# Thirty-two turns of the identity ahead of the input, the gate item in two products, one gate item in a bank of its own, and four changes of order

## The reference, cut to what matters

```python
def reference(x, mem, g_mix, w_in, b_igate, b_fgate, conv_w, conv_b, ...):
    ...
        xn = _rmsnorm(h, g_mix[l])
        proj = xn @ w_in[l]
        (sb_q, sb_k, sb_v, ml_q, ml_k, ml_v, ml_i, ml_f, ml_o, mem_q, gate_pre) = jnp.split(proj, splits, axis=-1)
        y_sb = _stick_breaking(...)
        qk = jax.nn.silu(_causal_conv(jnp.concatenate([ml_q, ml_k], axis=-1), conv_w[l], conv_b[l]))
        ...
        ig = (ml_i + b_igate[l]).astype(jnp.float32).transpose(0, 2, 1)
        lf = jax.nn.log_sigmoid((ml_f + b_fgate[l]).astype(jnp.float32)).transpose(0, 2, 1)
        hm = _mlstm(qh, kh, vh, ig, lf)
        ...
        gates = jax.nn.sigmoid(gate_pre + b_gate[l]).reshape(bsz, s, N_BRANCH, D_MODEL)
        ...
        h = h + merged @ w_out[l]
        hn = _rmsnorm(h, g_ffn[l])
        h = h + _peer(hn, w_peer_q[l], peer_k1[l], peer_k2[l], peer_u[l], peer_v[l])
```

## Time and profile before

| | us |
|---|---|
| median of 3 runs | 1645.74 |
| lowest, highest | 1645.55, 1647.4 |
| the profiled execution | 1646.79 |
| its span in the trace | 1645.1 |

### The profile page before, as it was taken

How to read it: one execution, slowest core, us unless ns; L and a number is a source line. 1 busy time by engine, 2 the same in 40 slices (tenths; PEclk the granted TensorE clock), 3 DMA queues, 4 the chain that set the end, 5 groups by cost and what they waited for, 6 DMA issues and landing times.

```text
span 1645.1 us, 23706 instructions
## 1 busy us (share of the span) xinstructions
PE 1629.1 (99%) x8192; PEld 1348.7 (82%) x8192; DVE 1085.2 (66%) x1884; ACT 755.4 (46%) x939; POOL 413.9 (25%) x180
## 2 busy tenths in 40 slices
...
DMA packets 165970, 344.39 MB, mean 209 GB/s; under 512 B 13068, under 2 KB 78604, under 8 KB 163600
## 3 DMA queue, kind: packets, MB, share of 16 engines
...
## 4 chain that ended last, share of the span: by engine, by line
PE 97%; DVE 1%; POOL 1%; DMA 0%; ACT 0%; issue 0%; SPq 0%; ACTq 0%
PE ps L971 28%; PE ps L962 27%; PE ps L634 19%; PE ps L647 9%; PE ps L885 4%; PE ps L1000 3%; PE ps L622 1%; PE ps L757 1%; POOL u_r L444 1%; PE ps L925 1%; PE ps L741 1%; PE ps L767 1%; PE ps L803 1%; PE ps L793 1%; PE ps L867 0%; PE ps L834 0%
## 5 line engine op out<-in xcount | busy, mean ns | idle before, releaser
L971 PE MATMUL ps<-v_r,w_pairs 128*128 128x512 f32 x2036 | 461.7, 389 | 0.0
L971 PEld LDWEIGHTS ps<-v_r,w_pairs 128*128 128x128 f32 x2036 | 382.1, 188 | 79.4
L962 PE MATMUL ps<-hT_r,u_r 128*128 128x512 f32 x1024 | 400.9, 391 | 0.5 <-POOL u_r L444 0.5
L962 PE MATMUL ps<-x_two,u_r 128*128 128x512 f32 x1024 | 398.7, 389 | 0.0
L419 POOL TENSOR_TENSOR w_r<-w_raw,w_r 128x1024 fp32r<-128x1024 f32 x93 | 234.8, 2527 | 396.1 <-ACT w_r L1097 390.3
L1903 DVE TENSOR_TENSOR v_r<-vraw,v_r 128x1024 fp32r<-128x1024 f32 x128 | 156.9, 1226 | 150.6 <-ACT v_r L1378 150.6
L1378 ACT ACTIVATE v_r<-vraw 128x1024 fp32r<-128x1024 f32 x128 | 135.7, 1060 | 253.9 <-PE ps L971 249.1
L634 PE MATMUL ps<-xT_r,w_r 128*128 128x512 f32 x984 | 230.2, 392 | 1.8 <-DVE xT_r L1419 1.0
L962 PEld LDWEIGHTS ps<-hT_r,u_r 128*128 128x128 f32 x1024 | 192.2, 188 | 41.2 <-POOL u_r L444 1.3
L962 PEld LDWEIGHTS ps<-x_two,u_r 128*128 128x128 f32 x1024 | 192.3, 188 | 39.4
L634 PEld LDWEIGHTS ps<-xT_r,w_r 128*128 128x128 f32 x984 | 182.9, 188 | 41.3 <-issue 2.4
...
## 6 DMA issues: line engine op xcount, KB each, us to landing
uraw<-in_u SPq DMA_DIRECT2D x128, 512.0 KB, 4.8
vraw<-in_v SPq DMA_DIRECT2D x128, 512.0 KB, 5.1
w_raw<-in_w SPq DMA_DIRECT2D x101, 512.0 KB, 3.5
acts_out<-act_stage SPq DMA_DIRECT2D x128, 256.0 KB, 2.3
...
act_in<-acts_out SPq DMA_DIRECT2D x128, 256.0 KB, 5.0
...
```

The lines of the kernel that those rows point to most:

```text
L962: ins = pe.matmul(bank(s % 2), u2[s][:, w, k * P:(k + 1) * P], x2[:, k, :] if w else hr4[:, 0, k, :], start=i == 0, stop=i == 15, skip_gro ...
L971: ins = pe.matmul(bank(2 * q + h), w2[:, s, w, q * P:(q + 1) * P], v2[s][:, w, h * BANK:(h + 1) * BANK], start=start and w == 0, stop=stop ...
```

## The change

Eight things change. `a`: ahead of the wait for x TensorE turns the identity 32 times into bank 7 (`WARM_TURNS`). `b`: the low part of item 0 is made by VectorE, behind the scaling of x, and both parts of item 1 by GpSimd, behind that; ScalarE no longer copies item 1. `c`: in item 16 GpSimd writes the low parts of the eight gate columns into unused columns (64 and 96 on) of the high part, so that high and low weights are one operand; TensorE does 16 matmuls in place of 24, and the sums over low weights come out in rows 64 to 67 and 96 to 99 of the same bank; ScalarE copies three rows of four out of the bank in place of one, and VectorE adds twice. `d`: the low part of item 17 is made by VectorE, ahead of the gate rows. `e`: the high part of item 19 is copied ahead of the Ln of the gate rows, not behind it. `f`: gate item 5 writes bank 6 and does not wait for item 4 to be taken out of bank 7. `g`: ScalarE takes an Exp of one column ahead of the first pair's scores, and the Exp of `r_m` stands behind the first pair. `h`: in the first `four_hots` the `low_u` stands behind all four groups of one-hots, not behind two. The other lines of the diff are counts and loops that follow from these.

```diff
+WARM_TURNS = 32
...
-DVE_LOW = tuple(I_KV + d for d in (1, 2, 4, 5, 7, 8, 10, 11))
+GATE_ASIDE = 5
...
+def gate_bank(m):
...
+    return 6 if m == GATE_ASIDE else 7
...
+DVE_LOW = (0, I_IF + 1) + tuple(I_KV + d for d in (1, 2, 4, 5, 7, 8, 10, 11))
...
-                        pool.wait_ge(w_hi_ready, o * 4 + (n + 1))
+                        pool.wait_ge(w_hi_ready, o * 4 + n)
...
-            low_ws(0, I_KV + 1)
+            pool.wait_ge(w_in[1], 16)
+            pool.wait_ge(w_lo_dve, 1)
+            pool.tensor_copy(wr4[:, 1, 0, :], raw3[:, 1, :]).then_inc(w_one_hi, 1)
+            pool.wait_ge(w_one_hi, 1)
+            pool.tensor_tensor(wr4[:, 1, 1, :], raw3[:, 1, :], wr4[:, 1, 0, :].bitcast(F32),
+                               ALU.subtract).then_inc(w_lo_ready, 1)
+            low_ws(2, I_IF - 2)
+            pool.wait_ge(w_hi_ready, I_IF)
+            raw_k = raw3[:, I_IF % 4, :].rearrange("p (k c) -> p k c", c=P)
+            hi_k = wr4[:, I_IF % 2, 0, :].rearrange("p (k c) -> p k c", c=P)
+            for i, done in ((0, if_low), (32, w_lo_ready)):
+                pool.tensor_tensor(hi_k[:, :, 64 + i:64 + i + MLH], raw_k[:, :, i:i + MLH],
+                                   hi_k[:, :, i:i + MLH].bitcast(F32), ALU.subtract).then_inc(done, 1)
+            low_ws(I_IF + 2, I_KV - 1 - I_IF)
...
-            with sp.Fori(1, I_IF // 4) as i:
+            for n in range(4, 8):
+                load_item(n, n % 4)
+            with sp.Fori(2, I_IF // 4) as i:
                 for s in range(4):
                     load_item(i * 4 + s, s)
-            for s in range(4):
-                load_item(I_IF + s, s)
-            with sp.Fori((I_IF + 4) // 4, (I_KV - 1) // 4) as i:
+            for n in range(I_IF, I_IF + 8):
+                load_item(n, n % 4)
+            with sp.Fori((I_IF + 8) // 4, (I_KV - 1) // 4) as i:
                 for s in range(4):
-                    load_item(i * 4 + s, s, 1)
+                    load_item(i * 4 + s, s, 1, 2)
...
             pe.wait_ge(const_set, CONSTS)
             pe.wait_ge(const_made, 4)
 
+            for i in range(WARM_TURNS):
+                turn(bank(7)[:, 0:P], ident[:, :])
...
             pe.wait_ge(proj_out, I_IF - 3)
-            t_item(I_IF, 0, 0, xr4)
+            take_item(I_IF)
+            pe.wait_ge(if_low, 1)
+            for k in range(KD):
+                for wa in range(2):
+                    ins = pe.matmul(bank(0), wr4[:, I_IF % 2, 0, k * P:(k + 1) * P], xr4[:, wa, k, :],
+                                    start=k == 0 and wa == 0, stop=k == KD - 1 and wa == 1)
+            ins.then_inc(item_done, 1)
...
-                at_least(pe, pre_out, m)
+                at_least(pe, pre_out, m - (m == GATE_ASIDE))
                 n = gate_at(m)
-                t_item(n, n % 2, 7, xr4)
+                t_item(n, n % 2, gate_bank(m), xr4)
...
             high_w(0, 0)
-            high_w(1, 1)
...
             act.wait_ge(item_done, I_N)
-            act.activation(r_zero, bank(0)[32:32 + MLH, :], ACT.Copy).then_inc(f_row, 1)
-            act.wait_ge(f_row, 1)
+            for dst, at in ((r_zero, 32), (r_f, 96), (r_max, 64)):
+                act.activation(dst, bank(0)[at:at + MLH, :], ACT.Copy).then_inc(f_row, 1)
+            act.wait_ge(f_sum, 1)
             link(act.activation(r_abs, r_zero, ACT.Abs, bias=bif[:, 1:2]))
             link(act.activation(r_abs, r_abs, ACT.Exp, scale=-1.0))
+            high_w(I_N + 2, (I_N + 2) % 4)
             act.activation(r_abs, r_abs, ACT.Ln, bias=1.0).then_inc(if_ln, 1)
             for b in range(4):
                 for j in range(4):
                     n = I_N + 4 * b + j + 2
-                    high_w(n, n % 4)
+                    if n > I_N + 2:
+                        high_w(n, n % 4)
                     if j >= 2:
...
                 for h in range(2):
                     act.wait_ge(act_step, steps[0] - 1)
                     step(act.activation(lk[h], lk[h], ACT.Exp, scale=-1.0))
-                if p == 0:
-                    act.wait_ge(rows_made, 1)
-                    act.activation(r_m, r_m, ACT.Exp, scale=-1.0).then_inc(thr_made, 1)
...
 
+            act.activation(roots[:, 61:62], eps_col[:, :], ACT.Exp)
             for p in range(PAIRS):
...
                 exp_part(2 * p)
                 exp_part(2 * p + 1)
                 high_ws(n + 2)
+                if p == 0:
+                    act.wait_ge(rows_made, 1)
+                    act.activation(r_m, r_m, ACT.Exp, scale=-1.0).then_inc(thr_made, 1)
...
             for i in range(TT):
                 dve.wait_ge(rooted, i + 1)
                 link(dve.reciprocal(rstd[:, i:i + 1], roots[:, i:i + 1]))
                 dve.tensor_scalar(xs3[:, i, :], xs3[:, i, :], rstd[:, i:i + 1], None, ALU.mult).then_inc(scaled, 1)
+            low_w(0)
             dve.wait_ge(params_in, 32)
...
+            low_w(I_IF + 1)
+            dve.wait_ge(f_row, 3)
+            dve.tensor_tensor(r_zero, r_zero, r_f, ALU.add).then_inc(f_sum, 1)
             dve.wait_ge(if_ln, 1)
             link(dve.tensor_scalar(r_f, r_zero, bif[:, 1:2], 0.0, ALU.add, ALU.min))
             dve.memset(r_zero, 0.0)
@@ -1458,14 +1504,9 @@
             link(dve.tensor_tensor_scan(r_b, r_lf, r_zero, 0.0, ALU.add, ALU.add))
             link(dve.scalar_tensor_tensor(out=r_a, in0=bank(0)[0:4, :], scalar=bif[:, 0:1], in1=r_b,
                                           op0=ALU.add, op1=ALU.subtract))
+            link(dve.tensor_tensor(r_a, r_a, r_max, ALU.add))
             link(dve.tensor_tensor_scan(r_max, r_a, r_a, 0.0, ALU.max, ALU.max))
             dve.tensor_tensor(r_m, r_b, r_max, ALU.add).then_inc(rows_made, 1)
...
-                dve.tensor_scalar(pre_stage[:, (m % 2) * T:(m % 2 + 1) * T], bank(7),
+                dve.tensor_scalar(pre_stage[:, (m % 2) * T:(m % 2 + 1) * T], bank(gate_bank(m)),
...
-            def four_hots(g, i, low):
+            def four_hots(g, i, low, behind=1):
 
                 for d in range(4):
                     one_hots(g + d, i + d)
-                    if d == 1:
+                    if d == behind:
                         low()
 
...
-            four_hots(0, 0, lambda: low_u(N_TOP, N_TOP % 4))
+            four_hots(0, 0, lambda: low_u(N_TOP, N_TOP % 4), 3)
```

19 lines of the change are left out of this document (10 added, 9 removed).

## The result

| | before | after |
|---|---|---|
| median of 7 runs, us | 1646.39 | 1640.61 |
| lowest, highest | 1645.55, 1647.4 | 1640.41, 1640.94 |
| profiled execution, its span | 1646.79, 1645.1 | 1640.6, 1638.9 |

The ratio is 0.9965, with a 95% interval of 0.9955 to 0.9975. The medians lie 5.8 us apart, and the sum of the prediction was 5.6. The predicted time, 1640.1, is half a microsecond low because it was taken from the median of the three runs shown, and with four more runs that median is 0.65 higher.

What follows compares the result with a forecast made beforehand. TensorE was taken to bound the kernel (97%). Terms of 1.7 + 1.8 + 1.3 + 0.9 - 0.1 = 5.6 us took the median of 1645.74 to 1640.1 us, range 1639.1 to 1642.7.

Steps and rivals of the forecast that it cites:

- The start: Up to item 0: early turns bring the fast pace before x, item 0 near 13.65; 1.7 us won, bounds 1.3 and 1.9.
- The gate item: Item 16: eight matmuls fewer win 1.8 us, kept if the items behind are ready; 0.1 us of wait booked at item 22.
- The shifted rows: Gate rows ahead of the first convolution: chain 3.4 us longer, but moving through GpSimd's subtractions, done at 17.9 instead of 16.5.
- the slack of 1.5 us: Item 22 before the change: GpSimd's low part ended at 25.7 after item 16, TensorE starting the item at 27.2.
- The aside: Gate item 5 and suffix sums: wait for bank 7 goes, `lk_hi` comes 1.8 us earlier; 1.3 us won, bounds 0.8 and 1.5.
- The rival with the wait for `lk_hi`: Suffix sums: gate item 5's wait returns whole as one for `lk_hi`, the table being loaded again; 1641.2 us, chance 0.06.
- The one-hots: Near 858 us: fourth group of one-hots ready without the wait, up-projections at 858.3 not 859.2; 0.9 us won, bounds 0.7 and 1.1.
- the case that ended slower: Items 17 to 32: VectorE does not catch up and TensorE waits 2.0 us in each of four blocks; 1648 us, chance 0.02.
- The pace did not fall: Start: rival that early turns bring no early clock, or it falls in the pause ahead of item 0; 1642.4 us, chance 0.10.
- everything between the places: Rest of the kernel outside the places read: TensorE runs back to back and moves with them, with no new wait.
- 1.4 us less gain: Whole kernel: the likeliest time's own bounds, 1.4 us less gain from the terms' ends and 0.6 more.

Runs made afterwards that it cites:

- three_products: Kernel after with gate item 16 in three products again (24 matmuls, one row copied out, no additions on VectorE): median 1642.06 us.
- no_aside: Kernel after with gate item 5 in bank 7 again, waiting for item 4 to be taken out, early Exp table load kept: median 1641.91 us.
- no_preload: Kernel after with the Exp table loaded between Abs and Exp again and the Exp of `r_m` between Exp and Ln: median 1641.98 us.
- hots_back: Kernel after with the low part of tile 56 behind the second group of one-hots again: median 1641.48 us.
- low17_gpsimd: Kernel after with item 17's low part made by GpSimd again: median 1641.52 us.
- trimmed: Kernel after with 24 identity turns for 32, item 22's copy ahead of `Silu`, item 67's copy ahead of the third branch-operand copy: median 1640.21 us.
- no_warm: Kernel after without its 32 turns of the identity, all else kept: median 1642.63 us.
- aside_alone: Kernel before with gate item 5 in bank 6 and nothing else: median 1645.92 us, ratio 0.9998.
- warm_12: Kernel after with 12 turns of the identity in place of 32: median 1641.95 us.

## Why the prediction was right

**The start.** Right, the size a little under. Three steps hold in the trace: the early turns, a fast pace before the first turn of x (from 7.92; predicted 7.4), and 1.99 us from the first turn of the last tile (11.41) to item 0, where 2.05 had been walked through. One did not hold in this execution: TensorE was to keep up with VectorE from the first tile on, and with the faster pace half a microsecond later than forecast its 64 turns ran without a wait, the last tile still 0.27 behind VectorE. That cost 0.16. It does keep up in three_products, no_aside, no_preload, hots_back, low17_gpsimd and trimmed, where item 0 comes 2.10 to 2.11 behind the last scaling. Item 0 was put at 13.65 and came at 13.40; with x landing alike in both, 1.66 to 1.81 were won against 1.7. The prediction read the 1.00 of the earlier trace rows as a granted clock that does not show the step; its reading of the slow pace as the 1.2 GHz level was right, and the 1.00 is no record at all, as the last section shows. The part that no row showed, GpSimd's copy, was taken at its upper bound of 2.36 and took 1.04, the lower end; nothing hung on it.

**What the early turns give.** Underrated by the medians. The prediction put the whole start on one execution's rise, 4.7 us after the first turn. By the medians no_warm, which keeps `b`, is 2.0 above the kernel after, more than the 1.7 booked for `a` and `b` together. The mechanism was right; its price varies with the execution.

**The gate item.** Right in each step. Sixteen matmuls took 3.63 us, 1.84 were won. The shifted rows went through GpSimd's subtractions much as walked: the first addition held (1.14 in place of 0.68), both scans in gaps, the second addition held, the convolution done 22.85 us behind item 16 against a forecast of 22.0 to 22.9, item 22's low part at 27.1 against 26.3 to 27.2, and a wait of 0.08 where 0.1 was booked. It was a narrow pass: the slack of 1.5 us was used up, and 0.1 beyond it. The walk took GpSimd's subtractions to stay where they are, and not all of them did: one took 3.23 us and one 3.01, each begun while VectorE was at work, but neither reached TensorE. `d` and `e` cover what was said: without them TensorE waits 0.6 and 1.9.

The Trainium skill (SBUF — State Buffer, Who interferes with whom) has a VectorE instruction with two inputs in SBUF and a GpSimd instruction that reads SBUF block each other wholly, by order of issue. The trace agrees: 1.21 for the free scan and 3.26 for the one begun inside a subtraction, in one kernel. The Trainium skill (DVE: opcode table, instruction layouts, handler registers and perf-mode slots, section 6) has the built-in scan run at half throughput; 1.21 against 0.68 for the plain addition of that size, somewhat under twice, agrees as well.

**The aside.** The step was right and the term mis-sized, 1.57 where 1.3 had been booked and 1.5 was the upper bound. Gate item 5 and its restart brought 1.1, as said; the suffix sums, whose waits for operands had been put at 0.2, brought 0.45. `lk_hi` began at 249.29, and its first half was done at 250.6, 0.6 before TensorE began on it at 251.24, where 0.5 had been reckoned. The preload fitted: Abs waited 0.28 for TensorE's scores and not the other way round. The rival with the wait for `lk_hi` is what aside_alone and no_preload show, 1.2 us; it did not come since one load of the table served both Exps.

**The one-hots.** Right: 1.10 won at the group, 0.2 given back ahead of tile 56, 0.82 against 0.9.

**The other rivals.** No block of items 17 to 32 but the first had a wait, so the case that ended slower did not begin. The pace did not fall in the idle 0.96 us ahead of item 0; warm_12 shows that it can fall, there behind an idle stretch of 2.7 us.

**What was missed.** The prediction called itself wrong if TensorE showed a wait at a place that it did not have before. It does, at the branch products, with 0.27 us. The step that failed is the sentence that everything between the places has TensorE back to back and moves with it. It moved with it but for one ScalarE instruction that began 0.28 later, in front of a chain with no slack. The reason lies in a count of instructions ahead of it, which neither the profile of before nor the order of work gives away.

**The level.** The forecast difference was right to 0.2 us (5.8 measured, 5.6 forecast). Some of this closeness is luck: the aside gave 0.27 more than booked and the branch products took 0.27 that nobody had booked, and the two cancel. The forecast time was 0.5 too low through the base that it was taken from. The prediction's "1.4 us less gain" is also more than its own ends give, 1.1 (0.4, 0.5 and 0.2); nothing hung on it.
